# Two blocks on one core: layers written out, products tile by tile across the norms, output gate and gate rows moved

## What is computed

```
h = rms_norm(x, g_pre_mix[l]);  z = h @ w_in[l]          # q, k, v, cb, cc, cx, ga, gb
y_attn = band_attention(rope(q), rope(k), v, sink) @ w_attn_proj
y_conv = (cb * short_conv(cc * cx)) @ w_conv_proj
x = x + rms_norm((sigmoid(ga) * y_attn + sigmoid(gb) * y_conv) @ w_out, g_post_mix)
h = rms_norm(x, g_pre_ffn)
x = x + rms_norm((silu(h @ w_gate) * (h @ w_up)) @ w_down, g_post_ffn)
```

```
h = rmsnorm(x) * (1 + scale) + shift
hh = num / max(|den|, exp(-m))
y = (rmsnorm(hh, hnorm_g) * sigmoid(o)) @ w_out;   x = x + g1 * y
```

## Time and profile before

| | us |
|---|---|
| median of 3 runs | 2707.39 |
| lowest, highest | 2698.58, 2713.43 |
| profiled execution, its own time | 2704.98 |
| its span | 2703.3 |
| PE busy | 2317.0 (86%) |
| DVE busy | 1724.4 (64%) |
| ACT busy | 969.1 (36%) |
| POOL busy | 681.8 (25%) |

### The profile page before, as it was taken

One profiled execution on the slowest core, in us unless ns is written; L12 is line 12 of the kernel. 1 busy time (PEld: TensorE's weight loads), 2 busy tenths in 40 slices (PEclk: granted clock), 3 DMA queues, 4 the chain that ended last, 5 costly groups with the idle time before them and its releaser, 6 DMA issues.

```text
span 2703.3 us, 34031 instructions
## 1 busy us (share of the span) xinstructions
PE 2317.0 (86%) x11772; PEld 1614.8 (60%) x11772; DVE 1724.4 (64%) x3318; ACT 969.1 (36%) x2084; POOL 681.8 (25%) x631
## 2 busy tenths in 40 slices
PE   7999899799989979898777789997788998677776
PEld 7999898699989968785232234454334446232222
DVE  5687677558668766457874464546864654955544
ACT  4434433443534344422232223522323632222222
POOL 0000001000000100003445433334532332455553
PEclk9999899899989989899989999999999999899999
DMA  7544477554547753149999999999999997999998
GB/s 294 191 167 182 179 275 284 200 224 156 189 155 270 275 208 125 63 168 366 388 383 421 422 416 393 407 394 385 394 424 385 393 392 310 373 396 422 421 421 343
DMA packets 110379, 828.24 MB, mean 306 GB/s; under 512 B 14368, under 2 KB 15280, under 8 KB 30848
## 3 DMA queue, kind: packets, MB, share of 16 engines
q0 software_dynamic: 90000, 595.97, 54.6%
q1 hardware_dynamic: 20208, 230.08, 22.3%
HBM read 824.95 MB, written 1.05 MB: 306 GB/s over the span
## 4 chain that ended last, share of the span: by engine, by line
PE 58%; DMA 17%; DVE 12%; ACT 5%; issue 4%; POOL 1%; ACTq 1%; DVEq 1%; PEldq 0%; POOLq 0%; SPq 0%; PEld 0%
PE pd L535 17%; PE pa L535 12%; PE pr L1018 11%; DMA ring_b<-in_peer_uv,eidx 9%; PE pr L535 8%; DMA wring<-in_peer_uv,eidx 7%; PE pa L1036 3%; DVE ring_b L2228 3%; PE pa L1130 2%; DVE wring L2228 2%; PE pd L1036 1%; ACT junk L1373 1%; DMA wring<-in_w_mix 1%; POOL ring_b L1571 1%; ACT gel L1367 1%
## 5 line engine op out<-in xcount | busy, mean ns | idle before, releaser
L1018 PE MATMUL pr<-ring_b,junk 128*128 128x512 f32 x1024 | 486.6, 622 | 136.6 <-ACT junk L1373 132.7
L1018 PE MATMUL pr<-wring,junk 128*128 128x512 f32 x1024 | 476.6, 612 | 128.0 <-ACT junk L1373 127.4
L1571 POOL DMA_INDIRECT ring_b<-in_peer_uv,eidx x256 | 312.7, 1222 | 676.8 <-PE pr L1018 414.9
L2228 DVE CUSTOM_DVE_ANT_0 ring_b<-ring_b,hrow 128x1024 f32<-128x1024 f32 x256 | 309.0, 1225 | 228.6 <-DMA ring_b<-in_peer_uv,eidx 222.0
L2228 DVE CUSTOM_DVE_ANT_0 wring<-wring,hrow 128x1024 f32<-128x1024 f32 x256 | 309.6, 1225 | 224.3 <-DMA wring<-in_peer_uv,eidx 218.3
L1018 PEld LDWEIGHTS pr<-ring_b,junk 128*128 128x128 f32 x1024 | 194.1, 198 | 413.5 <-issue 209.0
L1018 PEld LDWEIGHTS pr<-wring,junk 128*128 128x128 f32 x1024 | 191.1, 194 | 397.8 <-issue 203.0
L1571 POOL DMA_INDIRECT wring<-in_peer_uv,eidx x256 | 306.8, 1199 | 410.9 <-PE pr L1018 358.6
L1364 ACT ACTIVATE gel<-dots 128x2 f32<-128x2 f32 x256 | 51.9, 203 | 721.3 <-DVE dots L2228 719.9
L1558 POOL DMA_DIRECT2D aring<-in_ada_rows x112 | 60.2, 538 | 896.4 <-DVE adal L1641 896.2
L535 PE MATMUL pd<-hhi,wring_r 128*128 128x256 f32 x1024 | 224.1, 283 | 0.0
(11 more groups left out here) (363 smaller groups left out, 4204.8 us busy)
## 6 DMA issues: line engine op xcount, KB each, us to landing
wring<-in_w_mix SPq DMA_DIRECT2D x38, 2048.0 KB, 8.4
aring<-in_ada_rows POOLq DMA_DIRECT2D x112, 512.0 KB, 4.9
wring<-in_w_stick SPq DMA_DIRECT2D x24, 2048.0 KB, 9.7
wring<-in_w_ffn SPq DMA_DIRECT2D x22, 2048.0 KB, 8.3
wring<-in_w_lstm SPq DMA_DIRECT2D x12, 2048.0 KB, 7.9
wring<-in_w_back SPq DMA_DIRECT2D x8, 2048.0 KB, 8.2
wring<-in_w_back SPq DMA_DIRECT2D x4, 1536.0 KB, 6.8
ring_b<-in_peer_uv,eidx POOLq DMA_INDIRECT x256
```

Source lines behind the costliest of these rows:

```text
L1018: m = nc.tensor.matmul(pr[half][:, :], diag[:, q % DIAGS, :], row(q)[:, D + half * 512:D + (half + 1) * 512], start=(q % PICKS == 0), stop ...
L1571: pool.indirect_dma_start(out=row(q), out_offset=None, in_=ins["peer_uv"], in_offset=bass.IndirectOffsetOnAxis(ap=eidx[:, tt % NT, p:p + 1 ...
L2228: m = nc.vector.tensor_tensor_reduce(out=row(q)[:, 0:D], in0=row(q)[:, 0:D], in1=hrow[:, q // PICKS % NT, :], scale=1.0, scalar=0.0, op0=A ...
```

## The change

1. The loops over the layers are written out on all engines; waits compare with constants.
2. Down: the last four halves (TAIL) go tile by tile, tile 0's first, and the next layer's norm of tile 0 is transposed ahead of tile 1's last half. In the next layer slots 0 and 1 go tile by tile as well, hi products first, then those with the lower weights; tile 1's transposes stand ahead of tile 0's last piece. Rows scaled for this norm are kept in the place of `hlo`, since `x` and `xn` are in use.
3. The same between mixer and FFN: slot 19 goes tile by tile with 128 moving columns, tile 1's transposes between (in a bank of `pa`). And at the entry to the LSTM, for its slot 0.
4. On ACT and DVE casts, lower halves and the steps of the norms change places for this.
5. LSTM: gate pieces 0 and 1 go ahead of the heads. ACT takes exp(-o) out of PSUM, DVE adds 1 and takes the reciprocal, twice in the heads' loop, once behind it, once between the two tiles' rows. ROOTS' table is loaded after `num_ready`.
6. The gate rows g = 5 and 11 are made behind the heads, with g = 2.

```diff
@@ tensor
+            def rows_product_late(b, n, hi, lo, arrived, lower_there):
+                w_hi, w_lo = weights_of(n)
+                at = n % 2 * (COLS // 2)
+                for k in range(KC):
+                    arrived(k)
+                    for q, h in enumerate((hi, lo)):
+                        mm(b[:, at:at + COLS // 2], h(k), w_hi[:, k, :], start=(k == 0 and q == 0), stop=False)
+                lower_there()
+                for k in range(KC):
+                    m = mm(b[:, at:at + COLS // 2], hi(k), w_lo[:, k, :], start=False, stop=(k == KC - 1))
+                return m
...
-            with pe.Fori(0, DEPTH) as l:
+            for l in range(DEPTH):
...
                 for t in range(NT):
-                    norm_transposes(0, t)
-                for i in (Q_S, Q_S + 1, KV_S):
-                    banks = [bank_a(), bank_a()]
-                    for n in (2 * i, 2 * i + 1):
-                        split(n)
-                        for t in range(NT):
+                    for i in (Q_S, Q_S + 1):
+                        b = bank_a()
+                        for n in (2 * i, 2 * i + 1):
+                            if t == 0:
+                                upper_split(n)
+                            if l and t == 0 and n == 2 * Q_S + 3:
+                                norm_transposes(l, 0, 1, bank_d, pd_full)
                             arrived = half_tile(0, t) if n == 0 else lambda k: None
-                            m = rows_product(banks[t], n, tile_of(x_hi, t), tile_of(x_lo, t), arrived)
...
+                            m = rows_product_late(b, n, tile_of(x_hi, t), tile_of(x_lo, t), arrived, lower_there)
...
+                    for t in range(NT):
+                        for n in range(HALVES - TAIL, HALVES):
+                            if t == 0:
+                                split(n)
+                            elif n == HALVES - 1:
+                                norm_transposes(l + 1, 0, 0, bank_d, pd_full)
+                            down_product(n, t)
+                            if t:
+                                half_done(n)
...
+                def tile_products(b, n, c, t, lower_there):
...
+                    for g, k in steps:
+                        at = g * 256 + c * P
+                        for q, h in enumerate((hhi, hlo)):
+                            mm(out_of(g), w_hi[:, k, at:at + P], tile(h, k), start=(half == 0 and g == 0 and k == 0 and q == 0), stop=False)
+                    lower_there()
+                    for g, k in steps:
+                        at = g * 256 + c * P
+                        m = mm(out_of(g), w_lo[:, k, at:at + P], tile(hhi, k), start=False, stop=(half == 1 and g == 1 and k == KC // 2 - 1))
...
+            for p in range(AHEAD):
+                gate_piece(p)
             settle()
-
             pe.wait_ge(if_exp, 1)
...
+                if h > AHEAD:
+                    gate_piece(h - 1)
                 if h:
-                    gate_piece(h - 1)
                     lstm_values(h - 1)
             settle()
-            gate_row(2 * KC)
+            for g in (2, 5, 11):
+                gate_row(g * KC)
@@ scalar
-                for k in range(4):
+                for k in range(3):
                     row_square(1, k)
+                upper(l + 1, 0)
+                squares(2 * l + 2, 0)
+                upper(l + 1, 1)
+                if l + 1 < DEPTH:
+                    act.wait_ge(half_used, l * HALVES + HALVES - 1 + HI)
+                    tile_upper(l + 1, 0, 0)
...
+                row_square(1, 3)
+                upper(l + 1, 2)
+                upper(l + 1, 3)
+                squares(2 * l + 2, 1)
...
-                        nc.scalar.copy(so[:, t, p // 4 * 512:(p // 4 + 1) * 512], pd[(DEPTH * D_UNITS + u) % 2][:, :]).then_inc(pd_free, 1)
+                        nc.scalar.activation(so[:, t, p // 4 * 512:(p // 4 + 1) * 512], pd[(DEPTH * D_UNITS + u) % 2][:, :], ACT.Exp,
+                                             scale=-1.0).then_inc(pd_free, 1)
@@ vector
+                gained(1, 2)
+                dve.drain()
+                add_rows(1, 0)
+                lower(l + 1, 0)
+                normed_rows(2 * l + 2, 0)
+                if l + 1 < DEPTH:
+                    tile_raw(l + 1, 0, 0)
+                    tile_lower(l + 1, 0, 0)
...
+                lower(l + 1, 1)
+                gained(1, 3)
+                dve.drain()
+                add_rows(1, 1)
+                lower(l + 1, 2)
+                normed_rows(2 * l + 2, 1)
+                lower(l + 1, 3)
...
+            def gate_of(t, half):
+
+                v = so[:, t, half * 512:(half + 1) * 512]
+                dve.wait_ge(so_ready, 2 * half + t + 1)
+                nc.vector.tensor_scalar(v, v, 1.0, 1e38, ALU.add, ALU.min)
+                dve.drain()
+                nc.vector.reciprocal(v, v)
+                dve.drain()
...
+                if h in (4, 6):
+                    gate_of(h // 2 - 2, 0)
+            gate_of(0, 1)
```

More of the change, by code:

```diff
@@ L1174, in row_square @@
+            nc.scalar.preload_act_table_set(ROOTS)
+            for t in range(NT):
+                squares(0, t)
+            upper(0, 0)
+            tile_upper(0, 0, 0)
+            upper(0, 1)
+            upper(0, 2)
+            tile_upper(0, 0, 1)
+            upper(0, 3)
+            for l in range(DEPTH):
                 def row_square(n, k):
@@ L1629, in _, with take, lower, tile_raw @@
             dve.sem_inc(ada_free, 2)
-            with dve.Fori(0, DEPTH) as l:
-                nd = [0]
+            nd = [0]
+            def take():
+                u = nd[0]
+                nd[0] += 1
+                dve.wait_ge(pd_full, u + 1)
+                return pd[u % 2]
+            def lower(l, n):
+                dve.wait_ge(whi_ready, l * HALVES + n + 1)
+                lower_half(n)
+            def tile_raw(l, n, t):
+                cut = slice(t * P, (t + 1) * P)
+                for j in range(2):
+                    if n and t:
+                        u = (l + 1) * A_UNITS - 2 + j
+                        dve.wait_ge(pa_full, u + 1)
+                        b, freed = pa[u % 2], pa_free
+                    else:
+                        b, freed = take(), pd_free
+                    c, g = slice(4 * j, 4 * j + 4), (G_PRE, G_FFN)[n] + 4 * j
+                    gb = cols[:, g:g + 4].unsqueeze(2).to_broadcast([P, 4, P])
+                    nc.vector.tensor_tensor(hT[:, c, cut], b[:, :].rearrange("p (c n) -> p c n", c=4), gb, ALU.mult).then_inc(freed, 1)
+                    dve.drain()
+                    dve.sem_inc(h_raw, 1)
@@ new lines, in lstm_raw @@
+            def lstm_raw(t):
+                if t:
+                    u = DEPTH * A_UNITS
+                    dve.wait_ge(pa_full, u + 1)
+                    b = pa[u % 2]
+                else:
+                    b = take()
+                    nd[0] += 1
+                for c in range(4):
+                    nc.vector.tensor_scalar(hT[:, c, t * P:(t + 1) * P], b[:, c * P:(c + 1) * P], modA[:, 0, c:c + 1], shift(0)[:, c:c + 1],
+                                            ALU.mult, ALU.add)
+                dve.drain()
+                dve.sem_inc(h_raw, 1)
+                if t == 0:
+                    dve.sem_inc(pd_free, 1)
+                dve.wait_ge(hT_upper, t + 1)
+                if t == 0:
+                    dve.sem_inc(pd_free, 1)
@@ L1632, in _ @@
+            lower(0, 3)
+            tile_lower(0, 0, 1)
+            for l in range(DEPTH):
                 nada = [0]
```

547 lines of the change are left out of this document (274 added, 273 removed).

## The result

The changed kernel takes 2713.96 us (median of 20 runs, 2701.37 to 2732.06), the kernel before 2708.01 (20 runs, 2698.58 to 2713.73). The ratio is 1.0024, with a 95% interval of 1.0013 to 1.0035: slower by about 6 us, less than the half percent that the prediction took as the least that counts. I had forecast 2673. The profiled execution of the changed kernel took 2713.90, with a span of 2712.2.

What follows compares the result with a forecast made beforehand. PE bounds the layers and LSTM, DMA the last 1300 us of gathers, which can only start earlier. Terms -3.5 -18 -2 -4 -7 +5 -3 = -32.5 from 2705 give 2673 us; forecast 2666 to 2683, range 2656 to 2692.

Steps and rivals of the forecast that it cites:

- Norm to FFN, minus 1 each: Between mixer and FFN in each layer: idle filled with narrow products at 0.105 us; 1 us less each, 2 together.
- Rival (c): Three stages of narrow products run at the 1.2 GHz level, 0.214 us apiece: 63 us in all, 2736 us; chance 4%.
- Start, minus 3.5: Kernel start: PE's first product needs only tile 0's columns, split at about 16.1, so it starts 3.5 us earlier.
- Layer boundary, minus 18: Between the layers: tile 0 goes ahead of tile 1, so less idle and half pace on PE; 18 us less.
- 0.5 idle: Layer boundary: PE has products until T+8.3, tile 0's normed rows come at T+8.8, so it idles 0.5 us.
- Entry to the LSTM and heads, minus 11: LSTM entry tile by tile, minus 4 us; gate pieces filling the idle before the heads, minus 7 us.
- the heads start at 1070.4, but at the full clock: LSTM heads: start at 1070.4 instead of 1069.2, behind two gate pieces, without the 10 us at half pace.
- Tail, plus 5: LSTM tail: output gate's sigmoids move from ACT to DVE, with reciprocals of 3.3 us; 5 us more.
- Gate rows, minus 3: Two gate rows, 32 small matmuls in 3.83 us, leave the experts' first stage for the LSTM's tail; 3 us less.
- The gain up to the first gather is the gain at the end: Gather stage: keeps its length, so what PE gains before it moves everything after forward one for one; first gather some 31 us earlier.

Runs made afterwards that it cites:

- e5_fill: Changed kernel with tile 1's transposes ahead of tile 0's last 24 products in the first FFN slot, its columns ahead of a lower half on DVE; 2690.74 us.
- e4_three: Changed kernel with the first FFN slot wide again, two gate rows back in the experts' first stage, output gate a sigmoid on ACT; 2692.42 us, ratio 0.9952.
- e3_sigmoid: Changed kernel with the output gate as a sigmoid on ACT behind the heads, DVE's add and reciprocal gone; 2708.38 us, ratio 1.0006.
- e2_rows_back: Changed kernel with the two gate rows back in the experts' first stage; 2706.63 us, ratio 1.0006.
- e8: e4_three with FFN slot 24 of each layer, in a busy stretch, issued tile by tile in 192 products of 128 columns; 2741.64 us, ratio 1.0125.
- e7: e4_three with tile 1's columns ahead of the third lower half on DVE between mixer and FFN; 2690.64 us, ratio 0.9951.
- e11: Changed kernel with only the LSTM's slot 0 in wide products; 2718.21 us, ratio 1.0047.

## Why the prediction was wrong

- **"Norm to FFN, minus 1 each": the step that failed. "These products move 128 columns instead of 256", at 0.105, "the slot costs 20.2 us": the pace was right at full clock, the clock was the failure.** The measured 0.112 us would give 21.5 for the slot. The Trainium skill, "TensorE: Matmul & The Clock Gate", gives 107 ns for the load of 128 columns of weights (P/1.2, section "LDWEIGHTS (loading the stationary operand)"), and 56 ns for a 128-column matmul alone and 81 in a stream (section "Back-to-back issue gap"); the trace's 112 ns is nearest to the load. I worked only with the price at 2.4 GHz and had tile 1 done by 318.6, with nothing of the start's 3.3 us in it, so by 315.3; it was done at 324.58, and the slow wide products behind cost another 2 us. The measured changes are plus 10.4 and plus 9.5 in place of minus 1 each (my own working, 318.9 before against 318.6, gave no more than minus 0.3). Of the 36 us by which the first gather misses the sum (3.2 later in place of 32.5 earlier) these are 22: this step is what turned the gain into a loss. e5_fill shows it with a reordering that takes away the wait and leaves the work.
- **Rival (c) was the mechanism, and I gave it 4%.** My argument against it was that half pace was over 4 us after the products began. All those rows have 256 columns; under half clock narrow products start every 0.214, like wide ones, with the weight loads shown busy all the time, and in this slot they did not raise it. I had written down the very condition, "from the point where the clock falls at the transposes and doesn't come back within the slot", and had even worked out 2 us idle in the FFN's slot and 3 to 4 at the LSTM. The rows could not decide it, and I should have put it near even. Its 63 us was too much, since tile 0's half is ahead of the gap, and the LSTM's slot recovers in most profiles.
- **Start, minus 3.5:** right, 3.3, in part by luck. PE's first product comes 2.6 earlier (17.11 against 19.69). The rest agrees with the pace: before, the first products started every 0.214, now every 0.12, and the sum took nothing for that.
- **Layer boundary, minus 18:** 14.7. The step "0.5 idle" ahead of the transposes failed: it was 2.90. Not ACT's cast was late: ACT itself waited 2.59 us for DVE's residual (499.90). I had put gain and residual right behind the row's root, and left out DVE's last product for the modulation columns, which stands before them and waited 2.11 us for its rows; the residual was done 7.6 us after tile 0's last product (492.3) and not 3.7. In other profiles that product is done earlier against tile 0's last one, and the same wait of PE is shorter: 0.56 in e4_three, 1.13 in e3_sigmoid. In the changed kernel it brought half pace for eight transposes and six products.
- **Entry to the LSTM and heads, minus 11:** 3.1. The 0.31 us of waiting at 1071.51 is as forecast. But "the heads start at 1070.4, but at the full clock" failed: heads 0 to 2 have no piece left, with 28 matmuls in the 10 us from 1075, and the clock is down from 1073 to 1087. From the first head to the gate row it is 42.3 us, not 37.4. The entry itself gained about 1 and not 4: 141.96 from the down products to the first head against 141.71, with 5.8 of pieces put in and 4.99 of idle time gone. Some 40 of the slot's 192 narrow products ran at 0.214.
- **Tail, plus 5:** right, 5.3, with a reciprocal of 3.35 us where I took 3.3. The extrapolation from 2 and 8 elements held up to 512. The Trainium skill, "VectorE: DVE Perf Modes", section "First, the fixed hardware budget", led me to an estimate of 4.3 us from its repeat count of 8; the trace has 3.35, and the measurement decides.
- **Gate rows, minus 3:** wrong as a step of the sum: with the rows or without them it is 44.0 us from the transposes of the second block's rows to the first gather (e2_rows_back). I had counted PE's 3.8 us through in the same sentence that says that the first choice doesn't wait for them. The rows had covered a wait for modulated columns; PE stands 3.12 us there now.
- **"The gain up to the first gather is the gain at the end":** held within 1 us for e4_three against the changed kernel. For the changed kernel against the one before, 3.2 us at the first gather stand against 6 in the medians. The stretch behind the first gather took 1511 us in the one profile of before, 1511 to 1520 in the eight with the sigmoid and 1517 to 1521 in the five with the reciprocals. So 5.7 of the 8.9 us between the two profiled executions lie behind the first gather. Whether the reciprocals reach past it, by tile 1, stays open.

## What to carry to other kernels

Filling a gap with narrow products is no gain in itself: two products of 128 columns take 0.224 us for the work of one in 0.118, so what fills the wait is paid for in the next stretch. And a short wait in front of narrow products can cost as much as a long one in front of wide products, since in the FFN's slots the clock did not come back on them: look for the granted clock behind each remaining wait before counting its length. If a stretch must be narrow, let it begin and go on without a wait (e5_fill). Putting wide work behind the wait first may help too; that was not tried.

Work that looks free to move may be the cover of someone else's chain. Before taking it out, look at what the next instruction on that engine waits for and when that was done.

## What I had not expected of the hardware

- PE at 100% busy in the records for 38 and 40 us at a granted clock of 0.50 (e8, e7), with 128-column matmuls of 0.214 us; and 20 us of the same instructions at 1.00 in e8's layer 0. The work was the same; the difference that the rows show just before is the wait, 1.40 us (e8, layer 1) against 1.05 (layer 0).
- The LSTM's narrow slot was back at full clock 11 to 14 us in, behind eight transposes in its middle, in eight profiles, and in three, with the same transposes, it was not. The FFN's narrow slot, once fallen, never did: two layers each in the changed kernel, e2, e3 and e11, and e8's one. What tells these apart was not found.
- The clock fell 1 to 2 us after a wait of 2.00 us with eight transposes ahead of it (changed kernel) and after one of 1.40 us with none (e8), and it did not fall after one of 2.31 us with transposes and 512-column products behind it (e5_fill).
